# A sparse-attention phase with its normalising multiply on ScalarE, outputs split by head pair, and a final residual by tile

## The reference

```python
proj = rms_norm(h, g_mix_pre) @ w_in          # q, k, v of both attentions, an indexer, two gates
# stick-breaking attention, 8 heads of 64: a = sigmoid(z) * suffix product of (1 - sigmoid(z)),  o_sb = a @ v
# DSA, 8 heads of 64, per query the 256 best keys by the indexer's score:
p = jax.nn.softmax(logits, axis=-1);  o_ds = einsum('bhqk,bqkhd->bqhd', p, vg)
merged = gate_sb * (o_sb @ w_branch_sb) + gate_ds * (o_ds @ w_branch_dsa)
h = h + rms_norm(merged @ w_out, g_mix_post)
u = relu(rms_norm(h, g_mlp_pre) @ w1);  ff = (u * u) @ w2
h = h + rms_norm(ff, g_mlp_post)              # the result, without the meta tokens
```

## Time and profile before

| | us |
|---|---|
| median of 3 runs | 1873.12 (1873.09 to 1873.28) |
| profiled execution | 1872.9 |
| its span | 1871.1 |
| PE busy | 1771.6 (95%) |
| DVE busy | 1076.6 (58%) |
| ACT busy | 660.1 (35%) |
| POOL busy | 364.9 (19%) |

### The profile page before, as it was taken

How to read it: one execution, slowest core, us unless ns; L and a number is a source line. 1 busy time by engine, 2 the same in 40 slices (tenths; PEclk the granted TensorE clock), 3 DMA queues, 4 the chain that set the end, 5 groups by cost and what they waited for, 6 DMA issues and landing times. The chain is left out here.

```text
span 1871.1 us, 25716 instructions
## 1 busy us (share of the span) xinstructions
PE 1771.6 (95%) x10056; PEld 1502.7 (80%) x10056; DVE 1076.6 (58%) x1887; ACT 660.1 (35%) x1308; POOL 364.9 (19%) x160
## 2 busy tenths in 40 slices
PE   3999999999999999788999899999999999999996
PEld 3889888899888788677778688888888888888885
DVE  5277888999999996688954244322222222222236
ACT  5266444444444444566632232302111120203032
POOL 1112222321111111000014510404032231404030
PEclk9999999999999999898999899999999999999998
DMA  3565424423323322444124432202021211202032
GB/s 131 175 180 153 131 73 123 147 91 98 108 75 103 101 89 78 105 92 92 41 94 143 158 124 79 91 12 79 12 79 29 62 46 45 70 20 79 12 132 93
DMA packets 65471, 170.54 MB, mean 91 GB/s; under 512 B 9208, under 2 KB 23864, under 8 KB 65352
## 3 DMA queue, kind: packets, MB, share of 16 engines
q1 hardware_dynamic: 65352, 168.91, 30.0%
HBM read 126.47 MB, written 42.41 MB: 90 GB/s over the span
## 5 line engine op out<-in xcount | busy, mean ns | idle before, releaser
L593 PE MATMUL bk<-x_hi,w_hi 128*128 128x512 f32 (+2 forms) x832 | 309.0, 371 | 6.3 <-PEq L282 6.3
L593 PE MATMUL bk<-x_lo,w_hi 128*128 128x512 f32 (+2 forms) x832 | 298.7, 359 | 0.0
L593 PE MATMUL bk<-x_hi,w_lo 128*128 128x512 f32 (+2 forms) x832 | 297.9, 358 | 0.0
L263 POOL TENSOR_TENSOR w_lo<-w_raw,w_hi 128x1024 fp32r<-128x1024 f32 x53 | 131.4, 2479 | 484.2 <-ACT w_hi L259 484.2
L1352 ACT ACTIVATE relu<-bank 128x1024 f32<-128x1024 f32 x32 | 32.9, 1029 | 504.7 <-PE bank L1263 504.7
L1263 PE MATMUL bank<-m_hi,w_hi 128*128 128x512 f32 x512 | 199.5, 390 | 0.0
L1263 PE MATMUL bank<-m_hi,w_lo 128*128 128x512 f32 x512 | 199.2, 389 | 0.0
L1263 PE MATMUL bank<-m_lo,w_hi 128*128 128x512 f32 x512 | 199.2, 389 | 0.0
L914 DVE TENSOR_SCALAR_CACHE_REDUCE sel<-sc,st_bits 128x272 bf16<-128x272 f32 (+6 forms) x217 | 184.3, 890 | 0.9
L1433 DVE TENSOR_TENSOR acc<-acc,bank 128x1024 f32<-128x1024 f32 x56 | 68.3, 1220 | 188.4 <-PE bank L1239 187.6
L593 PEld LDWEIGHTS bk<-x_hi,w_hi 128*128 128x128 f32 x832 | 158.9, 191 | 22.1 <-POOL w_lo L263 6.4
(11 more groups left out here) (173 smaller groups left out, 3571.2 us busy)
## 6 DMA issues: line engine op xcount, KB each, us to landing
w_raw<-w_units SPq DMA_DIRECT2D x99, 512.0 KB, 3.7
raw<-w_units SPq DMA_DIRECT2D x24, 512.0 KB, 3.6
k_hi<-k_d SPq DMA_DIRECT2D x32, 260.0 KB, 5.3
k_lo<-k_d SPq DMA_DIRECT2D x32, 260.0 KB, 5.8
q_st<-q_d SPq DMA_DIRECT2D x32, 256.0 KB, 4.5
g_d<-stage_hi SPq DMA_DIRECT2D x32, 256.0 KB
gate<-g_d SPq DMA_DIRECT2D x16, 512.0 KB, 4.5
v_raw<-v_d SPq DMA_DIRECT2D x16, 260.0 KB, 7.3
```

The lines of the kernel that those rows point to most:

```text
L263: pool.tensor_tensor(w_lo[:, s], w_raw[:, s], w_hi[:, s].bitcast(F32), ALU.subtract).then_inc(lo_done, 1)
L593: mm = pe.matmul(pj[b][:, 0:c1 - c0], w[:, s, kt, :], a[:, kt, c0:c1], start=kt == 0 and k == 0, stop=kt == KT - 1 and k == 2)
```

## The change

In the DSA phase DVE keeps the reciprocal and ACT does the multiply: `normalise(j - 1)` stands in ACT's step in front of `round_weights(j - 2)` and `exponent(j)`. The outputs of DSA heads 8 to 13 are copied unsplit to `o_pair` (the space of the finished search), which frees the PSUM bank at once. When both heads of a pair are there, ACT rounds 128x1024 of it in one instruction (`round_pair`, steps 83, 99 and 115) and POOL makes the low part. Heads 14 and 15 are split by block as before. The low part of the four reloads goes from DVE to POOL.

In the closing stage the gain `g_fin` takes the place of the second gain once that is used up, and is loaded in front of most of the MLP's weights, the residual comes by tile, and POOL adds it for seven tiles; DVE does the eighth.

```diff
+PAIR_AT = [STEPS + 16 * (p_ + 1) + 3 for p_ in range(3)]
+PAIRED = STEPS + 48
...
+        o_pair = at("o_pair", [P, 3, SEQ], F32, O_SC)
...
+                for j in range(NJ // 2 + 1, NJ + 6):
+                    for p in range(4):
+                        if j == RELOAD[p] + 2:
+                            pool.wait_ge(or_hi, p + 1)
+                            pool.tensor_tensor(o_lo[:, p, :], o_raw[p % 2][:], o_hi[:, p, :].bitcast(F32), ALU.subtract).then_inc(or_lo, 1)
+                    for p in range(3):
+                        if j == PAIR_AT[p]:
+                            pool.wait_ge(op_hi, p + 1)
+                            pool.tensor_tensor(o_lo[:, 4 + p, :], o_pair[:, p, :], o_hi[:, 4 + p, :].bitcast(F32), ALU.subtract).then_inc(op_lo, 1)
...
+                def normalise(j):
+                    keys, s = KEYS[JOBS[j][2]], j % 2
+                    a = a_buf[:, j % 3, 0:keys]
+                    act.wait_ge(recip, j - NJ // 2 + 1)
+                    act.activation(a, a, ACT.Copy, scale=small[:, 24 + s:25 + s]).then_inc(a_done, 1)
...
+                    elif j < PAIRED:
+                        r = DH * (g % 2)
+                        if j == NJ // 2:
+                            act.wait_ge(mask_done, 1)
+                        act.copy(o_pair[r:r + DH, g // 2 - 4, i * P:(i + 1) * P], bk[o_bank(j)][0:DH, 0:P]).then_inc(o_free, 1)
...
+                def round_pair(p):
+                    act.wait_ge(o_free, STEPS + 16 * (p + 1))
+                    act.copy(o_hi[:, 4 + p, :], o_pair[:, p, :]).then_inc(op_hi, 1)
...
+                    if 1 <= j < NJ + 1 and JOBS[j - 1][0] == DS:
+                        normalise(j - 1)
...
+                    for p in range(3):
+                        if j == PAIR_AT[p]:
+                            round_pair(p)
...
+                    dve.sem_inc(mask_done, 1)
...
-                    dve.wait_ge(recip, e + 1)
-                    a = a_buf[:, j % 3, 0:keys]
-                    dve.tensor_scalar(a, a, small[:, 24 + s:25 + s], None, ALU.mult).then_inc(a_done, 1)
...
-                    dve.wait_ge(oh_done, j + 1 - NJ // 2)
+                    dve.wait_ge(oh_done, j + 1 - PAIRED)
...
-                    if 4 <= j and JOBS[j - 4][0] == DS:
+                    if j - 4 >= PAIRED:
                         rest_output(j - 4)
...
-        g_fin = at("g_fin", [P, D], F32, O_RB + 32768)
+        g_fin = at("g_fin", [P, D], F32, O_SEL + 4096)
...
+                sp.wait_ge(nn_done, NB)
+                sp.dma_start(g_fin[:], g_mlp_post.broadcast_to([P, D])).then_inc(gain_in, 16)
                 for v in range(U_MLP + 4, N_UNITS):
                     load_ring(sp, v)
...
-                sp.dma_start(g_fin[:], g_mlp_post.broadcast_to([P, D])).then_inc(gain_in, 16)
-                sp.dma_start(fin[:], h1_d.rearrange("(t p) d -> p t d", p=P)).then_inc(fin_in, 16)
+                for t in range(NB):
+                    sp.dma_start(fin[:, t], h1_d[t * P:(t + 1) * P, :]).then_inc(fin_in[t], 16)
...
+                for t in range(NB - 1):
+                    pool.wait_ge(fin_in[t], 16)
+                    pool.wait_ge(scaled_done, t + 1)
+                    pool.tensor_tensor(fin[:, t], fin[:, t], scaled[:, t % 2], ALU.add).then_inc(out_done, 1)
...
-                                dve.wait_ge(fin_in, 16)
+                                dve.wait_ge(m1_done, N1)
+                            if t >= 2:
+                                dve.wait_ge(out_done, t - 1)
                             dve.scalar_tensor_tensor(scaled[:, t % 2], acc[:, t], stat(11, t), g_fin[:], ALU.mult, ALU.mult).then_inc(scaled_done, 1)
-                            dve.wait_ge(scaled_done, t + 1)
-                            dve.tensor_tensor(fin[:, t], fin[:, t], scaled[:, t % 2], ALU.add).then_inc(out_done, 1)
+                            if t == NB - 1:
+                                dve.wait_ge(fin_in[t], 16)
+                                dve.wait_ge(scaled_done, t + 1)
+                                dve.wait_ge(out_done, t)
+                                dve.tensor_tensor(fin[:, t], fin[:, t], scaled[:, t % 2], ALU.add).then_inc(out_done, 1)
```

More of the change, by code:

```diff
@@ L446, in build @@
             or_in, or_hi, or_lo = [sem("f_orin0"), sem("f_orin1")], sem("f_orhi"), sem("f_orlo")
+            op_hi, op_lo, mask_done = sem("f_ophi"), sem("f_oplo"), sem("f_mask")
             block = st.enter_context(nc.Block())
@@ L1024, in rest_output @@
                     dst = (slice(r, r + DH), g // 2, slice(i * P, (i + 1) * P))
-                    dve.wait_ge(oh_done, j + 1 - NJ // 2)
+                    dve.wait_ge(oh_done, j + 1 - PAIRED)
                     dve.tensor_tensor(o_lo[dst], bk[o_bank(j)][0:DH, 0:P], o_hi[dst].bitcast(F32), ALU.subtract).then_inc(o_free, 1)
-                def rest_reload(p):
-                    dve.wait_ge(or_hi, p + 1)
-                    dve.tensor_tensor(o_lo[:, p, :], o_raw[p % 2][:], o_hi[:, p, :].bitcast(F32), ALU.subtract).then_inc(or_lo, 1)
                 for n in range(NC_STEP):
@@ L1074, in _ @@
                         spent += next(search, 1e9)
-                    for p in range(4):
-                        if j == RELOAD[p] + 2:
-                            rest_reload(p)
         gate = at("gate", [P, 2, 2, SEQ], F32, O_BACK)
@@ L1183, in build @@
             ysq, yvar, ystd, yrec, scaled_done, out_done = (sem("t_" + n) for n in "ysq yvar ystd yrec scaled out".split())
-            gains_in, gain_in, fin_in, stored_out = sem("t_gains"), sem("t_gain"), sem("t_fin"), sem("t_stored")
+            gains_in, gain_in, stored_out = sem("t_gains"), sem("t_gain"), sem("t_stored")
+            fin_in = [sem(f"t_fin{t}") for t in range(NB)]
             x_in = [sem("t_x0"), sem("t_x1")]
```

## The result

| | median us | lowest to highest, runs |
|---|---|---|
| before | 1873.2 | 1873.09 to 1874.13, 4 |
| after | 1851.02 | 1850.12 to 1851.17, 4 |

The profiled execution took 1850.96 us (span 1849.2).

What follows compares the result with a forecast made beforehand. DVE with its issue gaps was taken to bound a DSA head, PE close behind; in the closing stage DVE, held by the `fin` transfer, stalled PE. 1872.9 − 8.1 (tail) − 3.1 (DSA) = 1861.7, median 1862; range 1852 to 1869.

Steps and rivals of the forecast that it cites:

- Tail, -8.1: Closing stage: with the `fin` transfer off DVE's path and POOL adding seven tiles, PE sets the pace; 8.1 us saved.
- rival E: Closing stage: POOL and DVE hinder each other, so the gain there is only 4 us; total 1866, chance 0.05.
- The undisturbed head, 23.2: DSA phase: a head without disturbance takes 21.7 us of ACT plus 1.5 of uncovered waits, against 24.06 before.
- The gaps of 0.5: DSA head: half a microsecond of gaps added to ACT's 21.1 us busy, making 21.7.
- the three places: DSA head: uncovered waits at the longest row's scores (0.9), after the weight tiles (0.35) and after V tiles (0.25).
- +2.2 (+3.0 - 0.8): DSA phase: new pair casts on ACT cost 3.0 us; reload casts replacing DVE's subtractions as bound save 0.8.
- +1.1 for `v_raw`: First DSA head: the `v_raw` load waits behind a spill that ACT's output releases, now after the first multiply; 1.1 us.
- walked ACT's list alone: DSA head: time derived step by step from ACT's queue: output, multiply, casts, exponent; 23.2 us.
- rival B: DSA phase: ACT overlaps better and PE becomes the bound, 22.0 us a head; total about 1851.5, chance 0.2.
- C: DSA phase gains nothing, 23.6 us a head, as three engines are within 2 us; total 1865, chance 0.22.
- D: DSA phase: ACT is the longer chain, 26.2 us a head; total about 1884, chance 0.07.
- F: DSA phase: the exponent's table lacks the multiply, two table loads a step, 164 us longer; total 2030, chance 0.01.

Runs made afterwards that it cites:

- e16: The changed kernel with the seven 128x1024 rounding copies of the output part done by POOL instead of ACT: 1842.8 us.
- e13: The changed kernel with each of ACT's seven 128x1024 rounding copies done twice, first into a spare place: 1858.5 us.
- e4: The kernel before with only the closing-stage (tail) part of the change: 1864.9 us.
- e14: The changed kernel with DVE's subtraction for the last 16 outputs (heads 14 and 15) put ahead of the weights' subtraction: 1848.3 us.
- e2: The kernel before with only the multiply moved to ACT; old outputs, reload casts and tail: 1871.2 us.
- e11: The kernel before with the multiply on ACT and DVE's output subtraction, which releases the bank, put ahead of the weights' one: 1862.7 us.
- e9: The changed kernel with the multiply of each DSA head's longest block (1040 keys) given back to DVE: 1847.0 us.
- e3: The kernel before with outputs by pair and the reloads' low part on POOL; multiply still on DVE, old tail: 1862.5 us.
- e1: The kernel before with the whole DSA part of the change but the old closing stage: 1858.4 us.
- e12: The kernel before with only DVE's output subtraction, which releases the bank, put ahead of the weights' one: 1873.2 us.

## Why the prediction was wrong

**Tail, -8.1:** right, -7.8, and by the mechanism described: the transfer left DVE's path and PE set the pace. That POOL's additions cost DVE nothing (rival E) was luck in part: the reason given, that no row shows such a cost, was a misreading (above).

**The undisturbed head, 23.2: the step that failed.** e16 measures that head as 22.05: busy 20.5, where the prediction had 21.1, and 1.5 to 1.7 for all that is not busy. The multiply itself was priced right (0.77 forecast, 0.79 measured in the mean), but eight of them added 5.0 to 5.2 us of busy time (20.35 to 20.52 against the earlier trace rows's 15.32) and not 5.8, because ACT's instructions overlap by about 0.1 us when they stand in a row. Timeline of ACT of e16 in head 13:

```profile
869.86 1.16 ACT L789 ACTIVATE a_buf<-a_buf,small 128x1040 f32<-128x1040 f32 x1
870.93 0.73 ACT L798 CAST pt_hi<-bk 128x512 fp32r<-128x512 f32 x2
871.55 0.43 ACT L782 ACTIVATE a_buf<-n_buf,small 128x144 f32<-128x144 f32 x1
```

The cast starts 0.09 us before the multiply ends. DVE shows the same from the other side: it lost 5.5 us of busy time (21.89 to 16.35) and not 6.4. The gaps of 0.5 and the three places were counted one beside the other: 2.1, measured 1.6. These are two small errors on the same side, 0.6 and 0.5, in the difference of two numbers close to each other (24.06 and 23.2): the gain was 2.0 a head and not 0.85. In six heads: -12.1, forecast -5.1.

**The disturbed heads.** Six heads before took 154.54 us, six undisturbed ones would take 6 x 24.06 = 144.4. Of the 10.2 us between, 4.9 were the reload subtractions; the other 5.3 I left in place without a word. After, 138.46 - 6 x 22.05 = 6.2 us, for which e16 shows the seven copies as the cause. Forecast for this term was +2.2 (+3.0 - 0.8), measured -4.0: 6 us. The copies were priced nearly right, at 1 us each: 0.95 when added (e13), 0.75 when taken away (e16). What was missing are those 5.3 us, which went with the change. The clocks of 0.90 to 0.97 in these heads are a part of them, but how large a part is not shown, and one comparison speaks for a small one. Windows of head 12 of the kernel before and of e4, which has the same DSA code:

```profile
860.21:886.96 26.75, 23.07 (x210) 19.79 (x211) 23.12 (x70) 16.24 (x42) 0.00 (x0) 0.90 0.53 119
```

```profile
859.98:886.34 26.36, 22.30 (x210) 19.04 (x211) 23.11 (x70) 16.23 (x43) 0.00 (x0) 0.97 0.53 118
```

About half of the lowered stretch is missing in e4, and the head is 0.4 us shorter. The rest of the 5.3 would then be the standstills themselves: PE's waits for scores and for `o_lo` were 12.1 and 5.0 us before and are 5.7 and 0.5 after. That sum I did not separate.

**The two ends.** Head 8: forecast +1.1 for `v_raw` less half a head's gain, +0.7, measured -0.5; PE's wait for `v_raw` rose from 5.16 to 5.84 us. Head 15 was counted as a gaining head and is 2.3 us longer. Its outputs are still released by DVE. At full clock it is 27.21 us (e16), 0.9 more than before, and PE's waits for `o_lo` are there 2.8 us where they were 1.8; the other 1.4 go with the clock. With the swap (e14) it gains 1.2 on the kernel before. Terms together: -12.1 - 4.0 - 0.5 + 2.3 = -14.3; forecast -5.1 + 2.2 + 0.7 - 0.85 = -3.1.

**A gain that the forecast had by luck.** The forecast walked ACT's list alone. In e2 ACT has the same list but for the outputs, and heads 13 and 14, without a large copy, are 24.3 and 25.0 us (clocks 0.96 and 0.93), not 23.2: the walk fails there by 1 to 2 us on the other side. In e11, with the same instructions and the bank released early, they are 22.5 and 22.7 (0.99 and 1.00): PE's standstill for the output bank had returned to ACT as late transposes. I had the row (1.2 us for `o_lo`) and used it for rival B only. The early release, which the diff makes in passing by `then_inc(o_free, 1)` on ACT's copy, is what lets the two relieved engines meet: e2 to e11, 9.8 us.

**The rivals.** B (22.0 a head, fewer clock falls, total 1851.5) is nearest to what came, with a chance of 0.2 in the prediction. Its head is e16's 22.05. That its total fits to half a microsecond is luck: its "half hidden" copies cost 0.75 to 0.95 each, head 15 lost where B let it gain, and the disturbances gave more than it counted. The stated range says that it takes in B, yet it starts at 1852, half a microsecond above B's own figure. C, D and F are out: the phase gained, waits for the reciprocal are 1.7 us in six heads and not one in each step, and no table load stands between the exponents. (F's total should have read 2026, not 2030.)

## What to carry to other kernels

When work is taken off the bounding engine, list every semaphore that this engine gives to the others and where in its list each stands: once it has slack, the position of a release can be worth more than the time of the instruction (9.8 us for two exchanged calls; nothing measurable while the engine was full). Where three engines are within 2 us of each other, do not forecast from one engine's list with all uncertainties added on it; the range must reach down to the busy time of the next engine. And price disturbed stretches apart from undisturbed ones: here 5 us of them were a term of the sum, and were missing in it.

## What the runs showed of the hardware

- ACT's `Copy` with a [128,1] scale, SBUF to SBUF: 791 ns in the mean of 592 columns, within 1% of the exponent of the same form (1040 columns: 1.17 and 1.18 us), and no table load in between. The Trainium skill ("ScalarE: Activation LUTs", What ACT_TABLE_LOAD costs) gives an estimate of 0.77 us by its formula; the trace agrees within 3%. The same page's rule for kernel authors, to multiply on VectorE, held in part only: moved back for the longest block (e9) it gains 4 us, yet all of it on VectorE costs 3 (e3 against e1: phase 201.85 and 198.47).
- POOL rounds 128x1024 from SBUF as fast as ACT (1.04 and 1.05 us), while its subtraction takes 2.4. Group of POOL in e16, head 14:

```profile
L586 POOL CAST o_hi<-o_pair 128x1024 fp32r<-128x1024 f32 x1 | 1.0, 1043 | 37.0 <-ACT o_pair L820 37.0
```

- Beside one of POOL's two-operand instructions of 128x1024, a DVE addition of that size with one operand in PSUM stayed at 1.21 us, and a DVE subtraction with both operands in SBUF took 2.23 us for 1.23.
- Granted clock over heads 9 to 14: 0.94 before, 0.93 in e12, 0.96 in e3 and e4, 0.98 to 1.00 in all others. The four falls of heads 9 to 12 before came with a standstill of PE of 1.4 us in its wait for scores, but not each such standstill brings one. At 881.8 us the kernel before shows one of 1.41 us and the clock fell; e4 shows one of 1.40 us at the same place (881.5 us) and the clock did not fall until 3 us later. Which standstills cost the clock stays open, and so does what the falls cost: 0.4 us for half of one in head 12 (DVE full), 2.1 us for 0.98 against 0.87 in head 13 of e13.
